# Tables formed ahead of the weight stream, the order of the end, and an output pair ahead of the gated unit's products, in a two-block float32 kernel

## The chip, the cores and the metric

The program runs on one core of one Trainium2 chip. The metric is the device time of one execution in microseconds (us), the median of the runs shown. TensorE is called PE here, VectorE DVE, ScalarE ACT, GpSimd POOL and SyncE SP.

## The reference, cut to what matters

One sequence of 256 tokens with 1024 channels passes through a first block of two layers and a second block of one. All arithmetic is float32.

```
for layer in range(2):                       # first block
    xn = rms_norm(h, attn_norm_g); proj = xn @ w_in          # [256,1024] @ [1024,2304]
    u_ssm, u_g, v_g, q, k, v = split(proj, 256,256,256,512,512,512)
    y_ssm  = s5_mixer(u_ssm, ...)      # complex diagonal scan over tokens, GELU,
                                       # y * sigmoid(y @ w_glu + b_glu)  (the gated unit)
    y_sgu  = u_g * (W_s rms_norm(v_g) + b)                   # spatial gating
    y_diff = differential attention (q, k normed and rotated, 4 heads)
    h = h + concat(y_ssm, y_sgu, y_diff) @ w_out
    h = h + (gelu(conv3(gate)) * conv3(val)) @ w_down        # up 5632 wide, down 2816 deep
# second block
x = x + rms_norm((gates_a*ya + gates_b*yb + gates_m*ym) @ w_out, g_post)
# ya: attention over 3 dilated windows (24 heads, q and k rotated), yb: grouped attention,
# ym: attention over 256 memory rows; each times silu(gate) and a branch projection
```

## The kernel before, in words

**The stream.** The weights of both blocks are cut into chunks of 512 (or 256) columns and these into pairs, 294 in all, 512 KB each. A pair has a slot number p in `STREAM`: in layer 0 q has 0 to 3, k 4 to 7, ssm_u 8 and 9, gmlp 10 to 13, v 14 to 17, and the two output chunks 18 to 25 in turns. SP loads pair p into one of 7 `raw` buffers (L415) when pair p-7 has been used. ACT makes the high part of it (`whi`, L1068, `hi_upto(n)`: all up to pair n-1), DVE the low part (`wlo`, raw minus whi, L1662, `lo_upto(n)`), and PE then multiplies three products per piece: high by high, low by high, high by low (L534 to L536 where one token tile is done at a time, `tile_pairs`; L571 to L573 and L578 to L580 in `project`). PE waits for whi and wlo of each pair; `emptied(name)` waits until the PSUM bank of the chunk has been read out.

**The order.** Each engine runs one list in order, written out by hand; `hi_upto` and `lo_upto` are put between the other work. `link` on DVE and POOL makes the next instruction wait for the one before.

**The start.** POOL forms the scale of token tile t (`norm_rstd`, L1501 to L1503), DVE scales (`norm_scale`, L1671), PE transposes (L625), ACT and DVE write the high and low parts (`norm_hi` L1088, `norm_lo` L1680). PE does pairs 0 and 1 of q for tile 0, transposes the state matrices (L636, `b_transposes`), does pair 2, transposes tile 1, pair 3, and then q for tile 1, for which `norm_lo(0, 1)` must have run. Meanwhile DVE forms phases (L1716 to L1730, `phase_turns` L341 to L343), the rotation rows (`ropeq`, four instructions with `link`, L1773) and `coefficients` (L1740 to L1754). POOL forms powers of the decay (`amplitude_powers` L1526 to L1529), then `input_powers` (L395 to L398, for two halves c=0, 1), `head_powers` (L1537, L1538, L1490, L1491), `decay_table`, the identity sums and skip rows (L1558 to L1560, L1508; they overwrite the mask constants, so they wait for `maskb_ready`), `fold_coefficient` (L372 to L374) and `output_powers` (L383 to L385).

**The mixing of a layer.** PE: q, k, ssm_u, transposes of q heads (L730), `shuffle_in` (L668), `input_products` (L679, waits for ACT's `uc`), gmlp, transposes of k heads (L730, waits for DVE's scaled k, L1872), `scores(0)` (L744, L747), v, and so on. Then `output_products` (L689, L695; L689 waits for the transposed probabilities that ACT copies out, L1218), `shuffle_out`, `values`, `glu_products` (L717, the gated unit's), the output chunks.

**The second block.** In the rotations of six chunks (`rot_terms` on DVE L2120, two instructions per token tile; POOL adds them, L1628 and L1629; PE transposes the result, L965) and the branch attentions (ACT exponentials, DVE `branch_division` L2125 and L2127, PE transposes L936) the steps are placed by slot number n; `bm_slot(n, lag)` says whether attention step d has its stage with this lag at n. At the end PE does the branch chunks, transposes the first half of `merged` (L1035), does pairs 0 and 1 of wo0, transposes the second half, does pairs 2 and 3 of wo0, then wo1. DVE writes the low parts of the transposed `merged` (L2233, which PE's wo0 waits for), after the gating of the last branch (L2223, L2230). When the sums of squares are there, POOL forms the scale (L1502, L1503), DVE multiplies (L2245) and adds (L2250) and SP stores (L473).

Of the kernel before, what the change touches and what calls it, by code (L numbers as in the profile page):

```python
# [136 lines left out]
def build(nc, weights, x, mem, cols, rows, lams, bmerge, consts, amask, bexp, cexp, wst, wglu, out):  # L137
    with ExitStack() as ctx:
# [107 lines left out]
        st_ = sbt(mix, "st_", [P, 3, 8, 4])  # L246
        sv = qh[:, :, :, :].rearrange("p a b (s c) -> p (a b s) c", c=NC).rearrange("p (k s) c -> p k s c", k=4)
# [155 lines left out]
        def _(sp):  # L403
# [3 lines left out]
            n_par, n_id = COL["conv"][0], CST["ident"][1]  # L407
# [3 lines left out]
            for p, (nm, j) in enumerate(STREAM):  # L411
# [105 lines left out]
        def _(pe):  # L517
# [141 lines left out]
            for l in range(LAYERS):  # L659
# [186 lines left out]
                if l == 0:  # L846
# [106 lines left out]
            for c, nm in enumerate(A_CHUNKS):  # L953
                for j in range(4):
                    project(nm, pairs=[j], fm=nm == "ga")
                    if 1 <= c <= 6 and j >= 2:

                        rnd = 2 * (c - 1) + j - 2
# [3 lines left out]
                        for i in range(2):  # L962
                            f = 2 * (j - 2) + i
                            for t in range(TT):
                                m = pe.transpose(S1[:, i * TOK + t * P:i * TOK + (t + 1) * P], rt[:, t, f * P:(f + 1) * P], ident)  # L965
# [92 lines left out]
        def _(act):  # L1058
# [75 lines left out]
            act.wait_ge(sem("cst_landed"), 32)  # L1134
            act.copy(identb[:, :], ident).then_inc(sem("maskb_ready"), 1)
            for t, k in ((0, 4), (1, 2)):
                act.copy(maskb[:, t, :].rearrange("p (h n) -> p h n", h=k),
                         wide(cs("mdiff")[:, 0:128] if t == 0 else cs("mdiff")[:, 128:384], k)).then_inc(sem("maskb_ready"), 1)

            for l in range(LAYERS):  # L1140
# [32 lines left out]
                hi_upto(s0 + 17)  # L1173
                if l == 0:
                    phase_tables(act, 0)
# [1204 lines left out]
```

## Time and profile before

| what | us |
|---|---|
| median of 3 runs (1023.01, 1028.09, 1028.82) | 1028.09 |
| the profiled execution's own time | 1030.31 |
| span of its instructions | 1028.50 |
| mean granted clock of TensorE | 0.986 |

The span runs from the first to the last recorded instruction; the execution's own time is 1.81 us longer. Times in the rows are counted from the start of the span. A row of the timeline gives the start, the duration of the whole row (all its instructions), the engine, line, operation and tiles, the count (x3), and in brackets how long the engine sat idle before it and for what.

### The profile page before, as it was taken

What the parts mean: (1) busy time and instruction counts of PE and PEld (TensorE: products, weight loads), DVE (VectorE), ACT (ScalarE), POOL (GpSimd) and SP (SyncE); (2) the same over time, 40 slices, a digit from 0 to 9 for tenths busy, and PEclk for the clock granted to TensorE, in tenths of its full rate; (3) what the DMA queues carried; (4) which work ended last, traced back from release to release, by engine and by line L of the source; (5) the groups of instructions that cost most, each with busy time, mean ns of one, the idle gap of its engine ahead of it and who ended that gap; (6) DMA issues with size and microseconds to landing.
All of it is one profiled execution on the core that took longest, in us unless ns stands there. A gap on an engine that the chain in (4) does not pass through costs nothing.

```text
span 1028.5 us, 15910 instructions
## 1 busy us (share of the span) xinstructions
PE 988.0 (96%) x6210; PEld 862.9 (84%) x6214; DVE 703.5 (68%) x1072; ACT 547.7 (53%) x898; POOL 250.5 (24%) x196
## 2 busy tenths in 40 slices
PE   6979999999999999999999999999999999999986
PEld 4868889999977887889999888999767688888865
DVE  6998456699954688557787844648575755666955
ACT  7655545666654646546665634544445455555613
POOL 5880102588400021102435100012131300000210
PEclk9998899999999999999999999999999999999989
DMA  7632255556554543256655555565544445654541
GB/s 287 206 94 70 65 182 180 178 176 185 184 183 149 177 147 123 84 184 194 185 182 181 187 171 170 197 205 170 161 134 135 137 145 176 185 168 149 164 143 62
DMA packets 48474, 165.97 MB, mean 161 GB/s; under 512 B 6544, under 2 KB 7056, under 8 KB 48400
## 3 DMA queue, kind: packets, MB, share of 16 engines
q1 hardware_dynamic: 48400, 164.95, 50.6%
q8 instruction: 50, 0.82, 0.3%
q14 instruction: 24, 0.20, 0.1%
HBM read 162.83 MB, written 1.05 MB: 159 GB/s over the span
## 4 chain that ended last, share of the span: by engine, by line
PE 78%; DVE 13%; ACT 3%; issue 2%; POOL 2%; DMA 1%; SPq 0%; DVEq 0%; POOLq 0%; ACTq 0%
PE PJ L578 12%; PE PJ L580 11%; PE PJ L579 11%; PE PJ L571 10%; PE PJ L572 10%; PE PJ L573 10%; DVE wlo L1662 4%; PE PJ L534 2%; PE PJ L536 2%; PE PJ L535 2%; PE PJ L695 1%; ACT whi L1068 1%; DMA raw<-weights_in 1%; PE T L1009 1%; DVE xn L2120 1%
## 5 line engine op out<-in xcount | busy, mean ns | idle before, releaser
L1662 DVE TENSOR_TENSOR wlo<-raw,whi 128x1024 fp32r<-128x1024 f32 x294 | 377.6, 1313 | 125.1 <-ACT whi L1068 124.5
L1068 ACT ACTIVATE whi<-raw 128x1024 fp32r<-128x1024 f32 x294 | 303.4, 1061 | 71.5 <-DMA raw<-weights_in 65.3
L571 PE MATMUL PJ<-xth,whi 128*128 128x256 f32 x864 | 245.3, 284 | 1.7 <-DVE wlo L1662 0.9
L572 PE MATMUL PJ<-xtl,whi 128*128 128x256 f32 x864 | 244.5, 283 | 0.0
L573 PE MATMUL PJ<-xth,wlo 128*128 128x256 f32 x864 | 244.5, 283 | 0.0
L578 PE MATMUL PJ<-whi,xth 128*128 128x512 f32 (+1 forms) x432 | 176.2, 408 | 8.9 <-DVE wlo L1662 3.9
L580 PE MATMUL PJ<-whi,xtl 128*128 128x512 f32 (+1 forms) x432 | 168.8, 391 | 0.0
L579 PE MATMUL PJ<-wlo,xth 128*128 128x512 f32 (+1 forms) x432 | 168.6, 390 | 0.0
L571 PEld LDWEIGHTS PJ<-xth,whi 128*128 128x128 f32 x864 | 165.8, 192 | 2.6 <-issue 2.4
L572 PEld LDWEIGHTS PJ<-xtl,whi 128*128 128x128 f32 x864 | 165.8, 192 | 0.2
L573 PEld LDWEIGHTS PJ<-xth,wlo 128*128 128x128 f32 x864 | 165.8, 192 | 0.0
L1587 POOL TENSOR_TENSOR gtd<-acc 128x512 f32<-128x512 f32 x22 | 81.9, 3725 | 153.0 <-ACT acc L1294 149.7
L578 PEld LDWEIGHTS PJ<-whi,xth 128*128 128x128 f32 x432 | 82.0, 190 | 30.6 <-issue 11.7
L2001 DVE SCALAR_TENSOR_TENSOR acc<-PJ,colv,acc 128x255 f32<-128x255 f32 (+1 forms) x176 | 72.2, 474 | 48.8 <-ACT acc L1289 48.2
L580 PEld LDWEIGHTS PJ<-whi,xtl 128*128 128x128 f32 x432 | 82.1, 190 | 17.7
L1289 ACT ACTIVATE acc<-PJ,colv 128x256 f32<-128x256 f32 x88 | 42.6, 564 | 100.4 <-PE PJ L573 100.4
L579 PEld LDWEIGHTS PJ<-wlo,xth 128*128 128x128 f32 x432 | 82.4, 191 | 14.8
L578 PE MATMUL PJ<-whi,hth 128*128 128x512 f32 x144 | 57.2, 397 | 0.2 <-ACT whi L1068 0.2
L579 PE MATMUL PJ<-wlo,hth 128*128 128x512 f32 x144 | 57.1, 396 | 0.0
L580 PE MATMUL PJ<-whi,htl 128*128 128x512 f32 x144 | 57.1, 396 | 0.0
L1641 POOL TENSOR_TENSOR merged<-merged,gt 128x512 f32<-128x512 f32 x6 | 10.6, 1787 | 160.9 <-DVE gt L2223 160.9
L1078 ACT ACTIVATE sqs<-xres 128x512 bf16<-128x512 f32 x20 | 12.7, 633 | 38.8 <-DVE xres L1975 36.3
(398 smaller groups left out, 1399.6 us busy)
## 6 DMA issues: line engine op xcount, KB each, us to landing
raw<-weights_in SPq DMA_DIRECT2D x294, 512.0 KB, 3.5
rt<-bmerge_in SPq DMA_DIRECT2D x6, 256.0 KB, 4.0
xres<-x_in SPq DMA_DIRECT2D x2, 512.0 KB, 5.2
xn<-mem_in SPq DMA_DIRECT2D x2, 512.0 KB, 5.5
y_out<-xn SPq DMA_DIRECT2D x4, 256.0 KB, 2.4
rowv<-rows_in SPq DMA_DIRECT2D x1, 576.0 KB, 10.7
ptmp<-bexp_in SPq DMA_DIRECT2D x2, 256.0 KB, 6.1
cex<-cexp_in SPq DMA_DIRECT2D x2, 256.0 KB, 8.4
```

The lines of the kernel that those rows point to most:

```text
L534: pe.matmul(o, h, wh, start=(j == 0 and kk == 0), stop=False, skip_group_check=True)
L571: pe.matmul(o, a, xh[:, k, :], start=(first and f % 2 == 0), stop=False, skip_group_check=True)
L572: pe.matmul(o, a, xl[:, k, :], start=False, stop=False, skip_group_check=True)
L573: m = pe.matmul(o, b, xh[:, k, :], start=False, stop=last, skip_group_check=True)
L578: pe.matmul(o, h, wh, start=first, stop=False, skip_group_check=True)
L579: pe.matmul(o, h, wl, start=False, stop=False, skip_group_check=True)
L580: m = pe.matmul(o, lw, wh, start=False, stop=last, skip_group_check=True)
L1068: act.activation(whi[:, p % HIGHS, :], raw[:, p % LOADS, :], ACT.Copy).then_inc(hi_ready, 1)
L1289: act.activation(acc[:, j % 2, i, :], PJ[BUF[c]][:, i // 2, (i % 2) * TOK:(i % 2 + 1) * TOK], ACT.Identity, scale=colv[:, k + 2:k + 3], bi ...
L1587: pool.tensor_tensor(gtd[:, j % 2, :, :], acc[:, j % 2, 0:2, :], acc[:, j % 2, 2:4, :], ALU.mult).then_inc(sem("gated"), 1)
L1662: dve.tensor_tensor(wlo[:, p % LOADS, :], raw[:, p % LOADS, :], whi[:, p % HIGHS, :].bitcast(F32), ALU.subtract).then_inc(lo_ready, 1)
L2001: dve.scalar_tensor_tensor(out=acc[:, j % 2, i, sh:TOK], in0=PJ[BUF[c]][:, i // 2, (i % 2) * TOK:(i % 2 + 1) * TOK - sh], scalar=colv[:, k ...
```

## The change

It moves work, and changes the form of two steps. Nothing of the result is left out.
- The masks get a place of their own (in `kT`, loaded by one more DMA), so that POOL's identity sums and skip rows of layer 0 come first, before the powers.
- DVE of layer 0: phases and `phase_turns` come before the first scaling; rotation rows (`rotation_rows`) before `norm_lo(0, 1)`; `coefficients` before q's sums; the low parts of pairs are spread otherwise.
- POOL of layer 0: scale of tile 1 after `amplitude_powers`; fold and the first output powers before both `head_powers`.
- PE of layer 0: `b_transposes` after pair 0 instead of 1; gmlp pair 0 before `input_products`; `prob_transposes(0)` before pair 3 of v. ACT copies these probabilities out before the second exponentials.
- Both layers: pair 0 of the first output chunk before `glu_products`.
- Second block: `branch_division` before the low part and both tiles of `rot_terms` after it; PE transposes by token tile, so that the first tile needs half of the rotation.
- End: the low parts of the first half of `merged` before the last branch; wo0 as pair 0, transposes, pairs 1 to 3; DVE multiplies by `gpost` before the scale is there, and then scales and adds in one instruction.

```diff
@@ SP @@
-                    small(cst[:, n_id:NCST], consts[:, n_id:NCST], "cst_landed")
+                    small(cst[:, n_id:n_mask], consts[:, n_id:n_mask], "cst_landed")
+                    small(mdiff[:], consts[:, n_mask:NCST], "cst_landed")
@@ PE @@
-                    if l == 0 and j == 1:
+                    if l == 0 and j == 0:
                         b_transposes(0, B[:, 0, :])
...
                     shuffle_in()
+                    project("gmlp0", pairs=[0])
                     input_products()
-                    project("gmlp0", pairs=[0, 1])
+                    project("gmlp0", pairs=[1])
...
                     sgu_products()
+                    prob_transposes(0)
                     project("v0", pairs=[3])
-                    prob_transposes(0)
...
                 values(1)
-                glu_products()
                 out_terms = dict(ready=(sem("mix_lo"), 4 * l, 1), order=OUT_PAIRS)
                 project(f"out{l}_0", pairs=[0], **out_terms)
+                glu_products()
...
-                        pe.wait_ge(sem("a_rope"), 4 * c)
+                        pe.wait_ge(sem("a_rope"), 4 * c - 2 + 2 * t)
...
-            project("wo0", ready=(sem("m_lo"), 0, 1), pairs=[0, 1])
+            project("wo0", ready=(sem("m_lo"), 0, 1), pairs=[0])
             for f in range(4, KD):
                 merge_transposes(f)
-            project("wo0", ready=(sem("m_lo"), 0, 1), pairs=[2, 3])
+            project("wo0", ready=(sem("m_lo"), 0, 1), pairs=[1, 2, 3])
@@ ACT @@
+            b_evac(0, PJ[buf("k0")][:, 0, :])
             hi_upto(4)
-            b_evac(0, PJ[buf("k0")][:, 0, :])
...
                 hi_upto(s0 + 20)
+                if l == 0:
+                    prob_evac(0)
                 for c in range(2):
                     exps(1, c)
@@ POOL @@
             link(pool.memset(mT[:], 0.0))
-            norm_rstd(0)
+            norm_rstd(0, (0,))
+            pool.wait_ge(sem("ident_landed"), 16)
+            link(pool.tensor_tensor(skip[:, 0:64], ident[:, 0:64], ident[:, 64:128], ALU.add))
...
+            skip_rows(0)
             pool.wait_ge(sem("par_ready"), 3)
             amplitude_powers()
+            norm_rstd(0, (1,))
             pool.wait_ge(sem("bex_ready"), 1)
             input_powers(pool, link, 0, 0, x_tile(0), ptmp)
             input_powers(pool, link, 0, 1, x_tile(1), ptmp)
-            head_powers(0, 0)
...
-            folded(0)
+            pool.wait_ge(sem("par_ready"), 4)
+            fold_coefficient(pool, link, 0, ptmp)
+            output_powers(pool, link, 0, 0, ptmp)
+            head_powers(0, 0)
             head_powers(0, 1)
-            output_powers(pool, link, 0, 0, ptmp)
             output_powers(pool, link, 0, 1, ptmp)
@@ DVE @@
             dve.sem_inc(sem("par_ready"), 1)
+            link(dve.tensor_scalar(v[19], v[5], 2.0 / math.pi, None, ALU.mult))
...
+            phase_turns(dve, link, 0)
             norm_scale(0, xres, 0)
             lo_upto(1)
-            norm_lo(0, 0)
-            lo_upto(2)
             dve.wait_ge(sem("par_a"), 4)
...
+            norm_lo(0, 0)
             lo_upto(3)
             norm_scale(0, xres, 1)
             lo_upto(4)
-            link(dve.tensor_scalar(v[19], v[5], 2.0 / math.pi, None, ALU.mult))
...
-            norm_lo(0, 1)
-            lo_upto(7)
-            dve.wait_ge(sem("cst_landed"), 32)
+            dve.wait_ge(sem("cst_landed"), 48)
...
+            rotation_rows(0)
+            norm_lo(0, 1)
+            lo_upto(6)
...
+                    if bm_slot(n, 2) is not None:
+                        branch_division(bm_slot(n, 2))
                     lo_upto(F2 + n + 3)
                     if j == 0 and 1 <= c <= 6:
-                        rot_terms(c - 1, (0,))
-                    if bm_slot(n, 2) is not None:
-                        branch_division(bm_slot(n, 2))
-                    if j == 0 and 1 <= c <= 6:
-                        rot_terms(c - 1, (1,))
+                        rot_terms(c - 1, range(TT))
...
+                if i == 5:
+                    merged_lo(0)
+                    merged_lo(1)
                 lo_upto(min(end_pair(nm) + 3, FIRST[chunk("wo0")] + 3))
...
+                for t in range(TT):
+                    dve.wait_ge(sem("ssq_ready"), 24 + 2 * i + t + 1)
+                    dve.tensor_tensor(xn[:, t, half], PJ[buf(f"wo{i}")][:, t, :], gpost[:, half],
+                                      ALU.mult).then_inc(sem("wo_scaled"), 1)
...
+                        dve.scalar_tensor_tensor(out=xn[:, t, part], in0=xn[:, t, part], scalar=rstd[:, 6, t:t + 1],
+                                                 in1=xpar[t][:, part], op0=ALU.mult, op1=ALU.add).then_inc(sem("y_ready"), 1)
```

## Rows read from the trace of the kernel before

**Rows 1.** The page: busy time, share and count of each engine.
```profile
PE 988.0 (96%) x6210; PEld 862.9 (84%) x6214; DVE 703.5 (68%) x1072; ACT 547.7 (53%) x898; POOL 250.5 (24%) x196
```

**Rows 2.** Waits of PE: for whom; us in total, times, longest us.
```profile
PE PJ L578 <- DVE wlo L1662: 3.9, 3, 3.2
PE PJ L578 <- issue: 3.2, 1, 3.2
PE S L965 <- POOL rt L1629: 2.8, 2, 1.4
PE T L936 <- DVE sm L2127: 2.5, 5, 0.9
PE PJ L689 <- ACT pT L1218: 2.5, 2, 2.0
...
PE S L730 <- DVE xn L1872: 1.6, 1, 1.6
...
PE PJ L578 <- DVE xtl L2233: 1.0, 1, 1.0
...
PE T L679 <- ACT uc L1172: 0.7, 1, 0.7
```

**Rows 3.** Stretches: us; PE, PEld, DVE, ACT, POOL busy; PEclk; DMA share; GB/s.
```profile
70.00:76.00 6.00, 4.97 (x15) 3.52 (x16) 5.65 (x15) 3.32 (x15) 3.54 (x3) 0.72 0.08 9
...
96.00:112.00 16.00, 15.87 (x94) 14.75 (x94) 5.59 (x11) 8.29 (x17) 0.00 (x0) 0.58 0.00 0
404.00:419.00 15.00, 14.35 (x124) 12.77 (x124) 7.80 (x16) 13.61 (x27) 0.00 (x0) 1.00 0.12 36
...
995.00:1003.00 8.00, 8.00 (x27) 6.29 (x26) 0.00 (x0) 0.00 (x0) 0.00 (x0) 0.67 0.25 76
```

**Rows 4.** Timeline of DVE, 5 to 12 and 20 to 34 us.
```profile
7.62 0.88 DVE L1671 TENSOR_SCALAR xn<-xres,rstd 128x512 f32<-128x512 f32 x2 [2.61 <-POOL rstd L1503]
...
20.81 2.16 DVE L1680 SCALAR_TENSOR_TENSOR xtl<-T,colv,xth 128x128 fp32r<-128x128 f32 x8 [1.21 <-ACT xth L1088]
22.89 5.41 DVE L1662 TENSOR_TENSOR wlo<-raw,whi 128x1024 fp32r<-128x1024 f32 x3
28.21 5.42 DVE L1773 TENSOR_TENSOR ropeq<-cst,rowv 128x128 f32<-128x128 f32 x4
```

**Rows 5.** Timeline of ACT, 11 to 20 us, and of POOL, 20 to 34 us.
```profile
17.73 0.59 ACT L1099 COPY bex<-PJ 128x512 f32<-128x512 f32 x1 [1.70 <-PE PJ L636]
...
20.06 1.53 POOL L396 TENSOR_TENSOR vm<-bex,apw 128x768 f32<-128x768 f32 x1
...
27.17 2.52 POOL L396 TENSOR_TENSOR kmT<-bex,apw 128x768 f32<-128x768 f32 x1
...
31.30 1.85 POOL L398 TENSOR_TENSOR kmT<-kmT,ptmp 128x768 f32<-128x768 f32 x1
```

**Rows 6.** Timeline of DVE, 46 to 76 us.
```profile
53.25 0.69 DVE L341 TENSOR_TENSOR md<-sp_,chunks 128x512 f32<-128x512 f32 x1
...
54.44 0.69 DVE L343 SCALAR_TENSOR_TENSOR md<-md 128x512 f32<-128x512 f32 x1
...
67.40 2.98 DVE L1662 TENSOR_TENSOR wlo<-raw,whi 128x1024 fp32r<-128x1024 f32 x1
```

**Rows 7.** Timeline of PE, 66 to 71 us.
```profile
70.52 0.47 PE L578 MATMUL PJ<-whi,xth 128*128 128x512 f32 x1 [3.17 <-DVE wlo L1662]
```

**Rows 8.** Timeline of PE, 752 to 758 us, and of DVE there.
```profile
753.37 0.48 PE L578 MATMUL PJ<-whi,xth 128*128 128x512 f32 x1
...
757.75 0.44 PE L965 MATMUL S<-cst,rt 128*128 128x128 f32 x2 [1.39 <-POOL rt L1629]
...
751.48 1.64 DVE L2127 TENSOR_SCALAR sm<-sm,sx 128x256 f32<-128x256 f32 x2
```

**Rows 9.** Timeline of DVE, the end of the span.
```profile
1023.07 1.41 DVE L2245 SCALAR_TENSOR_TENSOR xn<-PJ,rstd,gpost 128x512 f32<-128x512 f32 x2 [2.64 <-POOL rstd L1503]
1024.40 1.28 DVE L2250 TENSOR_TENSOR xn<-xn,vm 128x512 f32<-128x512 f32 x2
```

More of the change, by code:

```diff
@@ L956, in _ @@
                     if 1 <= c <= 6 and j >= 2:
-                        rnd = 2 * (c - 1) + j - 2
-                        pe.wait_ge(sem("a_rope"), 4 * c)
+                        t = j - 2
+                        rnd = 2 * (c - 1) + t
+                        pe.wait_ge(sem("a_rope"), 4 * c - 2 + 2 * t)
                         if rnd:
                             pe.wait_ge(sem("a_ev"), rnd)
[L962 to L965, printed above, removed]
+                        for f in range(4):
+                            m = pe.transpose(S1[:, f * P:(f + 1) * P], rt[:, t, f * P:(f + 1) * P], ident)
                         m.then_inc(sem("a_tr"), 1)
@@ L1491, in power, with norm_rstd @@
                 pool.tensor_tensor(out_, out_, mhalf[:, 0:n], ALU.pow).then_inc(sem(signal), 1)
-            def norm_rstd(n):
+            def norm_rstd(n, tiles=range(TT)):
                 if n not in AT_ONCE:
@@ L1497, in norm_rstd @@
                     link(pool.tensor_scalar(ssm1[:, n, :], ssq[:, n, 0:4:2], D * EPS, None, ALU.add))
-                for t in range(TT):
+                for t in tiles:
                     pool.wait_ge(sem("ssq_ready"), 4 * n + (2 * t + 2 if n in AT_ONCE else 3 + t))
@@ L1710, in _ @@
             dve.sem_inc(sem("par_ready"), 1)
+            link(dve.tensor_scalar(v[19], v[5], 2.0 / math.pi, None, ALU.mult))
+            link(dve.tensor_scalar(v[18], v[19], MAGIC, None, ALU.add))
+            link(dve.tensor_scalar(v[18], v[18], -MAGIC, None, ALU.add))
+            link(dve.tensor_tensor(v[19], v[19], v[18], ALU.subtract))
+            link(dve.memset(chunks[:, :], 1.0))
+            link(dve.tensor_tensor_scan(chunks[:, :], chunks[:, :], chunks[:, :], -1.0, ALU.mult, ALU.add))
+            phase_turns(dve, link, 0)
             norm_scale(0, xres, 0)
             lo_upto(1)
-            norm_lo(0, 0)
-            lo_upto(2)
             dve.wait_ge(sem("par_a"), 4)
@@ L1771, in _ @@
                 s0 = slot(f"q{l}")
-                for i, (g, tb_) in enumerate((("qg", cosv), ("qg", sinv), ("kg", cosv), ("kg", sinv))):
-                    link(dve.tensor_tensor(ropeq[:, i, :, :], tb_, wide(row(g, 64 * l, 64), TT), ALU.mult))
+                if l:
+                    rotation_rows(l)
+                else:
+                    coefficients()
                 lo_upto(s0 + (9 if l else 7))
@@ L1867, in _ @@
                 if l == 0:
-                    phase_turns(dve, link, 0)
                     lo_upto(s0 + 13)
@@ L1937, in _ @@
                                                None, ALU.mult))
[L1938 removed]
+                if l:
+                    lo_upto(s0 + 21)
                 dve.wait_ge(sem("sgu_done"), l + 1)
@@ L2212, in _, with merged_lo @@
             output_lo(5)
+            def merged_lo(i):
+                dve.wait_ge(sem("m_hi"), i + 1)
+                dve.scalar_tensor_tensor(out=xtl[:, 2 * i:2 * i + 2, :], in0=AUX[i][:, :].rearrange("p (f n) -> p f n", f=2),
+                                         scalar=0.5, in1=xth[:, 2 * i:2 * i + 2, :].bitcast(F32),
+                                         op0=ALU.mult, op1=ALU.subtract).then_inc(sem("m_lo"), 1)
             for i, b in enumerate(BRANCH_ORDER):
@@ L2230, in _ @@
                         dve.tensor_tensor(m, m, gt[:, t, at_:at_ + 512], ALU.add).then_inc(sem("merged_ready_dve"), 1)
-            for i in range(4):
-                dve.wait_ge(sem("m_hi"), i + 1)
-                dve.scalar_tensor_tensor(out=xtl[:, 2 * i:2 * i + 2, :], in0=AUX[i][:, :].rearrange("p (f n) -> p f n", f=2),
-                                         scalar=0.5, in1=xth[:, 2 * i:2 * i + 2, :].bitcast(F32),
-                                         op0=ALU.mult, op1=ALU.subtract).then_inc(sem("m_lo"), 1)
+            merged_lo(2)
+            merged_lo(3)
             lo_upto(NPAIRS)
```

90 lines of the change are left out of this document (44 added, 46 removed).

## The prediction, made before the change was run

> **What bounds the kernel now.** I read the page's busy shares first: PE is busy for 988 of 1028.5 us, DVE for 68% [rows 1]. So only PE's idle time, and time in which PE runs at the lower clock, can be won. The waits of PE say where it idles [rows 2]: once 3.2 us for a low part of v's first pair, 2.0 for the transposed probabilities, 1.6 for the scaled k and 0.7 for `uc`, all in layer 0; 1.4 twice for a rotation and 0.95 twice for a division in the second block; 3.2 and 1.0 at the end. The stretches show the clock [rows 3]: 0.72 over 70 to 76 us, behind the wait of 3.17; 0.58 over 96 to 112, behind that of 2.0; 0.67 over 995 to 1003, behind that of 3.23 (1.2 GHz in part, 2.4 GHz in the rest). The same mixing stretch of layer 1, 404 to 419, had 1.00. Last come the timelines of DVE and POOL in the start, where the change moves most [rows 4, 5].
>
> **The change part by part.**
>
> *First scaling.* DVE sat idle for 2.61 us before 7.62 [rows 4]. It now gets six small instructions (some 1.4 us, by 0.2 each with their links) and `phase_turns`, 53.25 to 55.13 or 1.9 us [rows 6]. That is 3.3 in a hole of 2.6, and POOL's five small identity instructions come between, so that PE starts 0 to 1 late; I take 0.5. SP's added load costs its queue less than 1 us, ahead of pairs that are not due.
>
> *Rotation rows ahead of `norm_lo(0, 1)`.* This is the dear one. Before, the low parts of tile 1 began at 20.81 [rows 4] and PE's tile 1 just behind. The three low parts behind them took 5.41 where one takes 1.2, and the four rotation rows, 128x128 each, took 5.42, or 1.36 each. Beside them POOL ran `input_powers`, where an instruction took 1.53 alone and 2.52 beside a low part [rows 5]: the two engines take turns, one whole instruction each. A scaling by `tensor_scalar` is held up too: two of 128x256 took 1.64 [rows 8]. The change sends POOL into `input_powers` some 4 us earlier (amplitude powers need DVE's `par_ready`, now sent at 11 instead of 15; ACT's copy of the transposed state matrices, at 17.73 [rows 5], comes 2.4 earlier), at 16. That copy now stands ahead of the high part of pair 2, which I put at 16.8. Between this and `norm_lo(0, 1)` DVE has two low parts, two scalings and four rotation rows, 4.0 us of its own; POOL has six products of 1.53 to 1.85 and two copies of 0.4 less what is past, 9.6 us. By turns that ends at 16.8+4.0+9.6, or 30.4, against 20.81: 9.6 late, of which 0.2 may be hidden, so +9.4 for PE. The bounds: if DVE always came first, the rows would take 0.2 each and hide in the 1.21 us for which DVE waits for ACT there, so 0; if each of the eight DVE instructions met the longest whole turn, 8x1.85, or 14.8. I take 9.4, because rows 4 show turns wherever both were busy.
>
> The Trainium skill's page "SBUF — State Buffer", section "Who interferes with whom", says that a DVE instruction with two SBUF inputs and a GpSimd instruction that reads SBUF exclude each other for a whole instruction, and that the order of issue decides who waits. By it the sum could be 9.4 or near nothing, as the issues fall; the rows 4 and 5 show that it was DVE that paid on the long ones.
>
> *To the end of `scores(0)`.* It ended at 67.35, which is 70.52 less the wait [rows 7]. The wait for `uc` (0.7) is covered by gmlp pair 0, that for k (1.6) by DVE being rid of `phase_turns`: -2.3. DVE's chain from `norm_lo` on (two low parts, `coefficients`, sums, rotation, now beside POOL's output powers of some 2.5 us each) brings the low part of pair 9 about 1.5 late: +1.5. PE will also stand idle for 4 to 5 us before tile 1, longer than any pause that lowered the clock before, and PE has 24 wide products then; after 3.23 us the clock stayed low for some 6 us, after 3.17 for some 3 [rows 3], so I give +1 here, less than they cost there since DVE sets the pace behind it. With the 0.5 of the start and the 9.4, `scores(0)` ends 10.1 later, at 77.4.
>
> *From `scores(0)` to the output.* The wait of 3.17 for the low part of v's first pair goes: DVE's low part that took 2.98 beside POOL [rows 6] is done before `scores(0)` ends. What is late next is the low part of pair 15, behind `batch_max(0)` and the lambdas: +1.6. The 2.01 for the probabilities goes, since ACT copies them before the second exponentials, which wait for DVE anyway. With no pause ahead of the narrow products the clock should stay at 2.4 GHz, as in layer 1: 16x(1-0.58), or 6.7, and 6x(1-0.72), or 1.7, are won [rows 3]; 1.1 comes from small waits and issue gaps between. Sum -3.2-2.0-6.7-1.7-1.1+1.6, or -13.1. Bounds: -5 if the clock falls all the same, -16 without the new wait and with 0.7 of gaps more.
>
> *Output pair ahead of the gated unit.* Both need `g_ready`, the bank's release as much as the products, so PE waits for nothing new. The gated unit ends 2.8 us later; its result is due at the output pair with `mix_lo` 2, but DVE's `diff_norm(0)`, which stands between and waits for POOL, is not done earlier anyway. 0 in each layer, -0.4 to +1.5.
>
> *Second block.* At chunks 2 and 5 the division came behind a `rot_terms` and was held up by POOL; now ACT's exponentials are done before the low part's own wait ends. The transposes for tile 0 need only POOL's first half. PE's products that began at 753.37 could have begun at 751.8, and the transposes at 757.75 at 756.2 [rows 8]: 3.1, twice, -6.2. Bounds -5.1 (the recorded waits 0.95, 0.23 and 1.39 alone, twice) and -6.4. The division now waits for ACT ahead of the low part; DVE was idle for ACT there. Without that cover it would cost 1.0 in each of twelve places, of which PE sees none while low parts run two pairs ahead.
>
> *End.* PE began wo0 3.23 late; now its first low part is written before DVE's last two of the stream, and pair 0 covers the gating of the last branch (2.6 us for 2.8 of products). The wait goes, the 0.98 for the second half too, and the clock: 8x(1-0.67), or 2.6, and 0.3 before 995. Sum -7.1 [rows 2, 3]. Bounds -4 (a gap of some 1.5 stays and costs some clock) and -7.3.
>
> *Tail.* Behind the last scale DVE had four instructions, 1023.07 to 1025.68 [rows 9]; now two of 0.64 to 0.68: -1.3 (-0.6 to -1.4).
>
> Sum: +10.1-13.1+0-6.2-7.1-1.3 is -17.6. From the profiled execution's 1030.31 that is 1012.7; the median of the runs stands 2.2 lower, so I say 1010.5.
>
> **The rivals.** *The turns cost nothing* (chance 0.27). DVE's instructions slip in between POOL's and the rotation rows hide. For it: the fifteen small `coefficients` ran unhindered beside POOL's small ones; against it: rows 4. Then +9.4 and the clock's +1 and the +1.5 go: 1010.5-11.9, or 998.6.
>
> *The mixing's clock falls anyway* (chance 0.12). PE's narrow products behind `output_products` keep the clock down whatever is before them. Against: layer 1's 1.00 [rows 3]. Then 8.4 stay: 1018.9.
>
> *Slower: the pause at the start brings the clock down for the whole of k and ssm_u* (chance 0.04). PE then does some 25 us of products at 1.2 GHz, +25 less 6 that the DVE chain hides there: 1029.5; it decides the sign from about 18 us at the lower clock on. For it: no pause in the trace is as long as this one; against: after every pause of rows 3 it came back within 3 to 15 us.
>
> **How the numbers follow.** My forecast has 0.57. The time is the likeliest's, 1010.5. The range reaches from the first rival's 999 to the second's 1019, and leaves out some 0.15. A measurement here tells about 1% from no change: faster by over 1% (below 1017.8) takes the forecast, the first rival and a part of the second, 0.91; within 1% 0.06; slower 0.03.
>
> **What would show each step.** Right: PE's wait at tile 1's first product of q for DVE's xtl, 5 us or more, with rotation rows of 1 us and more beside `input_powers`; no wait for the low part of v's first pair; clock 1.00 over the narrow products; no wait of 3 us at wo0; no waits for division and rotation at chunks 2 and 5. Wrong: rotation rows of 0.2 each (first rival), or a clock of 0.6 in the mixing (second).

## The result, and the profile after

The changed kernel took 1013.58 us in the median of 4 runs (1013.32 to 1013.89), the kernel before, beside it, 1028.45 (1023.01 to 1029.48): a ratio of 0.987, 95% interval 0.983 to 0.990. The profiled execution took 1013.32, with a span of 1011.5 and a mean clock of 0.995. It is faster by over 1%, as forecast, 3.1 us slower than the number forecast, and inside the range.

The page's busy times first, to be read beside [rows 1].

```profile
PE 977.9 (97%) x6214; PEld 855.5 (85%) x6214; DVE 706.6 (70%) x1072; ACT 547.6 (54%) x898; POOL 244.2 (24%) x196
```

PE is busy for 10.1 us less with the same products: that is time at the lower clock. The other 7 of the 17 us of the profiled executions are idle time. Which, the waits of PE show (us in total, times, longest), beside [rows 2]:

```profile
PE S L627 <- DVE xn L1680: 11.7, 6, 9.6
PE PJ L536 <- DVE xtl L1689: 5.4, 2, 4.2
PE PJ L536 <- issue: 3.1, 2, 2.4
PE PJ L580 <- issue: 2.0, 4, 0.6
PE PJ L580 <- DVE wlo L1671: 1.6, 2, 1.4
...
PE PJ L691 <- ACT pT L1221: 0.5, 1, 0.5
```

The groups of [rows 2] for the rotation, the division, the scaled k, `uc` and `merged` are gone. New are 4.2, 2.4 and (in a group of its own) 1.3 in the start, 1.4 for a low part at v's second pair, and two gaps a layer, 2.0 in all, of the group "L580 <- issue". The stretches answer to [rows 3]: us; PE, PEld, DVE, ACT and POOL busy; granted clock; DMA share; GB/s.

```profile
78.00:94.00 16.00, 14.62 (x91) 12.01 (x90) 15.37 (x34) 9.41 (x30) 2.13 (x2) 1.00 0.33 106
94.00:110.00 16.00, 15.66 (x129) 13.57 (x128) 8.29 (x19) 12.49 (x29) 0.00 (x0) 1.00 0.11 34
402.00:417.00 15.00, 14.20 (x123) 12.68 (x122) 8.15 (x16) 13.60 (x26) 0.00 (x0) 1.00 0.11 36
...
985.00:993.00 8.00, 8.00 (x40) 6.58 (x40) 6.47 (x8) 5.82 (x7) 0.00 (x0) 1.00 0.47 172
...
36.00:40.00 4.00, 4.00 (x19) 3.32 (x18) 3.01 (x9) 1.25 (x2) 2.22 (x3) 0.98 0.78 262
32.00:36.00 4.00, 4.00 (x11) 3.03 (x11) 3.76 (x11) 1.06 (x1) 0.00 (x0) 0.50 0.26 82
28.00:32.00 4.00, 1.30 (x3) 1.10 (x4) 3.93 (x10) 0.38 (x1) 2.77 (x5) 0.67 0.01 2
```

The narrow products of layer 0 (94 to 110) now run at 2.4 GHz, and so does the end; at the lower clock are now the first products of tile 1, from 30.7 to some 36 us. Their cause stands in the timelines of PE, DVE and POOL there (start, duration, and in brackets the idle time before), beside [rows 4, 5]:

```profile
19.86 0.47 PE L536 MATMUL PJ<-whi,xth 128*128 128x512 f32 x1 [2.37 <-issue]
30.70 0.79 PE L536 MATMUL PJ<-whi,xth 128*128 128x512 f32 x1 [4.24 <-DVE xtl L1689]
...
8.90 0.93 DVE L1680 TENSOR_SCALAR xn<-xres,rstd 128x512 f32<-128x512 f32 x2 [0.46 <-POOL rstd L1510]
19.68 3.70 DVE L1680 TENSOR_SCALAR xn<-xres,rstd 128x512 f32<-128x512 f32 x2
24.66 5.35 DVE L1747 TENSOR_TENSOR ropeq<-cst,rowv 128x128 f32<-128x128 f32 x4
30.04 2.16 DVE L1689 SCALAR_TENSOR_TENSOR xtl<-T,colv,xth 128x128 fp32r<-128x128 f32 x8
45.83 1.21 DVE L1800 TENSOR_TENSOR qh<-PJ,ropeq 128x1024 f32<-128x1024 f32 x1
48.09 3.21 DVE L1671 TENSOR_TENSOR wlo<-raw,whi 128x1024 fp32r<-128x1024 f32 x1
...
23.61 2.51 POOL L397 TENSOR_TENSOR kmT<-bex,apw 128x768 f32<-128x768 f32 x1
26.09 1.56 POOL L398 TENSOR_TENSOR ptmp<-bex,apw 128x768 f32<-128x768 f32 x1
27.73 1.80 POOL L399 TENSOR_TENSOR kmT<-kmT,ptmp 128x768 f32<-128x768 f32 x1
...
44.78 2.97 POOL L385 TENSOR_TENSOR ptmp<-gpw,apw 128x1024 f32<-128x1024 f32 x1
```

The rotation rows took 1.34 each beside POOL's big products, and tile 1's low parts began at 30.04 instead of 20.81.

How the same points of PE's work moved between the two traces gives the account. A sum of the differences is the whole change of the profiled execution, 1030.31 to 1013.32.

| stretch | point at its end on PE, before and after | change in the stretch | forecast |
|---|---|---|---|
| first scaling | first product, 11.58 and 12.63 | +1.05 | +0.5 |
| to tile 1 | its first product, 21.47 and 30.70 | +8.18 | +9.4 |
| to `scores(0)` | its last product, 67.35 and 76.83 | +0.25 | +0.2 |
| mixing of layer 0 | first transposes of the next stage, 139.02 and 137.09 | -11.41 | -13.1 |
| layer 0's rest, layer 1's mixing | 432.86 and 431.55 | +0.62 | 0 |
| second block | `merged`'s transposes, 984.57 and 976.25 | -7.01 | -6.2 |
| end | last product, 1021.02 and 1005.26 | -7.44 | -7.1 |
| tail | own time, 1030.31 and 1013.32 | -1.23 | -1.3 |

### The profile page after: what moved, and what is told of

Read it like the earlier page. It is cut to its first block, busy times and chain, and to the rows that moved or that the text cites. A ratio compares the mean times of both kernels' runs of the same rounds, so it can differ in the third digit from the quotient of the medians.

```text
span 1011.5 us, 15918 instructions
## 1 busy us (share of the span) xinstructions
PE 977.9 (97%) x6214; PEld 855.5 (85%) x6214; DVE 706.6 (70%) x1072; ACT 547.6 (54%) x898; POOL 244.2 (24%) x196
## 3 DMA queue, kind: packets, MB, share of 16 engines
HBM read 162.83 MB, written 1.05 MB: 162 GB/s over the span
## 4 chain that ended last, share of the span: by engine, by line
PE 86%; DVE 7%; issue 2%; ACT 2%; POOL 1%; DMA 1%; DVEq 0%; POOLq 0%; SPq 0%; ACTq 0%
PE PJ L580 14%; PE PJ L582 13%; PE PJ L581 13%; PE PJ L573 10%; PE PJ L574 10%; PE PJ L575 10%; PE PJ L536 2%; PE PJ L538 2%; PE PJ L537 2%; DVE wlo L1671 2%; PE T L1011 1%; DVE xn L1680 1%; PE PJ L697 1%; PE T L1002 1%; PE T L775 1%
## 5 line engine op out<-in xcount | busy, mean ns | idle before, releaser
L580 PE MATMUL PJ<-whi,xth 128*128 128x512 f32 (+1 forms) x432 | 174.3, 403 | 3.9 <-issue 2.0
L580 PEld LDWEIGHTS PJ<-whi,xth 128*128 128x128 f32 x432 | 81.2, 188 | 24.9 <-issue 8.2
L580 PE MATMUL PJ<-whi,hth 128*128 128x512 f32 x144 | 57.2, 397 | 0.2 <-ACT whi L1070 0.2
L536 PE MATMUL PJ<-whi,xth 128*128 128x512 f32 x64 | 27.3, 426 | 8.5 <-DVE xtl L1689 5.4
```

The costliest lines, as they stand in the source:

```text
L536: pe.matmul(o, h, wh, start=(j == 0 and kk == 0), stop=False, skip_group_check=True)
L580: pe.matmul(o, h, wh, start=first, stop=False, skip_group_check=True)
```

## Experiments

The first eight kernels and `tail_back` start from the changed kernel or from `rot_late`; the last three build on what these showed. Where nothing else is said, each computes the whole reference.

### What the start costs: start_before

```diff
-            phase_turns(dve, link, 0)
             norm_scale(0, xres, 0)
...
+            norm_lo(0, 1)
+            lo_upto(7)
             dve.wait_ge(sem("cst_landed"), 48)
...
-            rotation_rows(0)
-            norm_lo(0, 1)
-            lo_upto(6)
```

and all else that the change moved ahead of `scores(0)` put back on PE, ACT, POOL and DVE. The masks keep their own place.

> The changed kernel with the start of the kernel before (order of DVE, POOL and ACT up to scores(0), transposed state matrices after pair 1, both gmlp pairs behind the input products); the mixing from scores(0) on, the output pair, the second block, the end and the tail stay changed. In the profile of the changed kernel PE does its first product of tile 1 at 30.70 us instead of 21.47, and ends scores(0) near 76.8 instead of 67.35. Theory (the new start costs and nothing behind needs it): scores(0) ends near 67.4 again, the time falls by about 9, less what comes back (3.2 for the low part of v's first pair if phase_turns in k's way makes it late again, with some 2 of clock behind it): 1004 to 1010. Rival (what the start costs it gives back later: rid of the start's tables DVE and ACT are ahead in the mixing): 1013 or more, with the waits for the low part of v's first pair and for the probabilities back and the clock down over the narrow products.

Measured: 1007.93 us (1007.84 to 1008.61), ratio 0.980 (0.977 to 0.984); 5.6 less than the changed kernel. The timeline of PE in it:

```profile
59.44 0.77 PE L732 MATMUL S<-cst,xn 128*128 128x128 f32 x5 [1.74 <-DVE xn L1881]
70.71 0.77 PE L580 MATMUL PJ<-whi,xth 128*128 128x512 f32 x1 [3.17 <-DVE wlo L1667]
```

`scores(0)` begins at 66.07 instead of 75.14, 9.1 earlier; the waits of 1.74 and 3.17 are back, and its stretch 70 to 76 had a clock of 0.50. By the first transposes after the output the lead is 4.9 (132.22 against 137.09). So the theory holds and the rival holds in part: the new start costs 9.1, and gives back 4.2 behind it. Many steps were put back at once here; the next kernels take single ones.

### Which instruction pays for POOL: rot_late and powers_wait

rot_late:

```diff
-            rotation_rows(0)
             norm_lo(0, 1)
             lo_upto(6)
+            rotation_rows(0)
```

> The changed kernel with the four rotation rows moved behind the low parts of tile 1 and of pairs 4 and 5, where POOL has finished input_powers. In the changed kernel they take 5.35 us at 24.66, beside POOL's input_powers, and PE waits for the low parts behind them. Theory (turns: each of the four waits for one whole POOL product): norm_lo of tile 1 starts 4 to 5 earlier, PE's wait there shrinks by as much, the rows take 0.2 to 0.4 each where POOL is done, and the time falls by 3 to 5, to 1008.5 to 1010.5. Rival (the price is POOL's, whatever DVE does there: the eight low parts of tile 1 are then held up by the same POOL products, by some 5 us): tile 1 is no earlier by more than 1 us and the time stays at 1013.

Measured: 1013.14 (1012.64 to 1013.56), 0.4 less than the changed kernel. The timelines of PE and DVE in it:

```profile
52.29 0.45 PE L573 MATMUL PJ<-xth,whi 128*128 128x256 f32 x1 [2.92 <-DVE wlo L1671]
...
24.89 2.15 DVE L1689 SCALAR_TENSOR_TENSOR xtl<-T,colv,xth 128x128 fp32r<-128x128 f32 x8
45.62 2.47 DVE L1805 TENSOR_TENSOR xn<-qh,sm 128x512 f32<-128x512 f32 x1
48.01 2.87 DVE L1806 TENSOR_TENSOR xn<-qh,sm 128x512 f32<-128x512 f32 x1
```

Neither theory gave this. The low parts of tile 1 were 5.2 earlier and PE's 4.24 were gone, as the theory of turns said, and the eight of them were not held up (2.15 beside a product of POOL from 23.85 to 26.35), against the rival; the time hardly moved, because DVE, now earlier in q's work, did two rotations beside POOL's output powers (2.47 and 2.87, where the same took 0.68 and 0.71 in the changed kernel), and PE waited 2.92 at ssm_u instead.

powers_wait:

```diff
             pool.wait_ge(sem("bex_ready"), 1)
+            pool.wait_ge(sem("xt_lo"), 16)
             input_powers(pool, link, 0, 0, x_tile(0), ptmp)
```

> The changed kernel with one wait added: POOL starts input_powers when the low parts of tile 1 are written (xt_lo 16). Nothing is left out. DVE then has no POOL product beside its scaling of tile 1, low parts of pairs 2 and 3 and rotation rows. Theory (turns): the four rotation rows take some 0.2 to 0.3 us each instead of 1.34, DVE's wlo pairs 1.2 instead of 2.0, tile 1's low parts start 5 to 7 us earlier, PE's wait of 4.24 goes; input_powers ends some 5 us later, which k's transposes and DVE's coefficients may feel. Time 1006 to 1010. Rival (rotation rows are slow by themselves, 128x128 with a broadcast operand): they still take 1.3 each with POOL idle, and the time stays within 1 us of 1013.5 or rises, since the powers are later.

Measured: 1015.23 (1013.07 to 1016.47), 1.7 more than the changed kernel; three of the four runs lie above all of its runs, one below. Its timelines of DVE and PE:

```profile
20.97 1.26 DVE L1748 TENSOR_TENSOR ropeq<-cst,rowv 128x128 f32<-128x128 f32 x4
27.34 1.46 DVE L1758 TENSOR_TENSOR sp_<-colv 128x16 f32<-128x16 f32 x1
...
40.27 0.77 PE L580 MATMUL PJ<-whi,xth 128*128 128x512 f32 x1 [4.13 <-DVE wlo L1672]
```

With POOL idle the four rotation rows took 1.26 together, 0.31 each: the 1.34 of the changed kernel is POOL's price, and the mechanism is shown. But the time did not fall, and in the median it rose. The `coefficients` behind them, 128x16 and 0.17 each in the changed kernel, now stood beside `input_powers`, and six of them took 1.41 to 1.67; PE then waited 4.13 and 3.11 for low parts of k and ssm_u. The turns were not saved but paid by the next in DVE's queue.

### The output powers: rot_late_heads_first

```diff
             input_powers(pool, link, 0, 1, x_tile(1), ptmp)
+            head_powers(0, 0)
...
             fold_coefficient(pool, link, 0, ptmp)
-            output_powers(pool, link, 0, 0, ptmp)
-            head_powers(0, 0)
             head_powers(0, 1)
+            output_powers(pool, link, 0, 0, ptmp)
```

on top of rot_late.

> As rot_late (rotation rows behind the low parts of tile 1), and POOL's head powers ahead of the decay table and of the output powers again, as in the kernel before. In rot_late the wait of 4.24 at tile 1 was gone, and 2.92 came at 52.29 us for a low part of ssm_u, behind a low part of 2.83 and two rotations of 2.47 and 2.87 which DVE did beside POOL's output powers. Theory (POOL's big products cost DVE their turns wherever they stand, and the output powers stand in q's way there): the rotations take 0.7 each, the wait at ssm_u goes or is under 1, and the time falls by 3 to 5 from 1013.1, to 1008 to 1010. Rival (DVE is late by its own work, with coefficients and phase_turns ahead of q's sums): the wait at ssm_u stays over 2 and the time is above 1012.

Measured: 1007.58 (1006.75 to 1008.50), ratio 0.981 (0.977 to 0.985), 5.6 less than rot_late. Its timeline of DVE:

```profile
42.86 0.70 DVE L1805 TENSOR_TENSOR xn<-qh,sm 128x512 f32<-128x512 f32 x1
43.48 0.69 DVE L1806 TENSOR_TENSOR xn<-qh,sm 128x512 f32<-128x512 f32 x1
```

The rotations are short, and no wait of 0.3 or more is left on PE between 25 and 72 us. The output powers, which began at 42.64 in rot_late, began at 55.16 here: ahead of the head powers they put POOL's longest products beside DVE's work on q. With the rotation rows already moved, taking them away won 5.6, and the whole price of the start is gone (start_before took 1007.93). The head powers' order without rot_late's edit was not run, so how the price divides between the two is not shown; rot_late alone won only 0.4.

### One pause and the narrow products: probs_late

```diff
-                    prob_transposes(0)
                     project("v0", pairs=[3])
+                    prob_transposes(0)
...
-                if l == 0:
-                    prob_evac(0)
                 for c in range(2):
                     exps(1, c)
-                if l:
-                    hi_upto(s0 + 21)
-                    prob_evac(0)
-                    hi_upto(s0 + 22)
+                hi_upto(s0 + 21)
+                prob_evac(0)
+                hi_upto(s0 + 22)
```

> The changed kernel with the transposed probabilities put back in layer 0: PE transposes them after pair 3 of v, ACT copies them out after the second exponentials. Theory (one pause of PE ahead of the narrow products brings the clock down for them): PE waits 1.5 to 2.5 us before output_products and the granted clock over the next 16 us falls to 0.55 to 0.8, so that the time rises by 2 plus 3 to 7: 1018 to 1022. Rival A (the clock needs the longer wait for v's first pair too, which stays away): the wait of about 2 comes back, the clock stays at 1.00, 1015.5. Rival B (ACT is early enough now that even the old order waits for nothing): 1013.5.

Measured: 1020.73 (7 runs, 1015.51 to 1022.41). PE's timeline and the stretch behind, of the profiled execution (1021.41):

```profile
99.65 0.52 PE L691 MATMUL PJ<-uc,mT 128*128 128x64 f32 x3 [2.01 <-ACT pT L1221]
```

```profile
99.00:115.00 16.00, 15.35 (x89) 14.84 (x91) 3.76 (x7) 8.27 (x16) 0.00 (x0) 0.57 0.01 1
```

The wait is the 2.01 of before, and the clock falls to 0.57 where the changed kernel has 1.00: the theory. What it did not foresee is that this is not so in each execution. Of the seven, five took 1020.5 to 1022.4 with a mean clock of 0.988 to 0.991, and two took 1015.5 and 1016.1 with 0.997: 2.2 us above the changed kernel, as the wait of 2.01 alone would give. None of the other six executions was traced; that the clock fell in four of them and stayed up in two is read from the mean clock.

### The output pair: glu_first

```diff
                 out_terms = dict(ready=(sem("mix_lo"), 4 * l, 1), order=OUT_PAIRS)
-                project(f"out{l}_0", pairs=[0], **out_terms)
                 glu_products()
+                project(f"out{l}_0", pairs=[0], **out_terms)
```

> The changed kernel with the gated unit's products ahead of the first output pair again, in both layers. In the changed kernel PE has two new gaps a layer, 0.34 and 0.64, at 109.32 and 115.12 and again at 414.97 and 420.77, and between 403.83 and 431.55 it loses 1.05 us against the kernel before. Theory (the swap costs about 1 us in each layer: the low part of the gated unit's result is later and the output pairs behind it wait): both gaps go in both layers and the time falls by 2 to 1011.6. Rival (the gaps belong to something else, the order of the low parts or the earlier probabilities in layer 0): they stay and the time is within 0.4 of 1013.6; then layer 1, where only the swap differs, should show them still.

Measured: 1011.50 (5 runs, 1011.21 to 1012.20), 2.1 less than the changed kernel, whose four runs lie in 1013.32 to 1013.89. First the changed kernel, layer 1, PE and ACT; then glu_first:

```profile
414.97 0.47 PE L580 MATMUL PJ<-whi,xth 128*128 128x512 f32 x1 [0.34 <-issue]
417.80 1.89 PE L719 MATMUL PJ<-md,wglus 128*128 128x256 f32 x8
420.77 0.47 PE L580 MATMUL PJ<-whi,xth 128*128 128x512 f32 x1 [0.64 <-issue]
...
419.73 0.84 ACT L1267 ACTIVATE md<-PJ,hb 128x256 f32<-128x256 f32 x2 [2.65 <-PE PJ L719]
```

```profile
416.33 0.59 PE L580 MATMUL PJ<-whi,xth 128*128 128x512 f32 x1
419.64 0.47 PE L580 MATMUL PJ<-whi,xth 128*128 128x512 f32 x1
...
416.91 0.85 ACT L1267 ACTIVATE md<-PJ,hb 128x256 f32<-128x256 f32 x2
```

The gaps go in both layers, and 403.8 to 431.55 shrinks by 1.08. The pair at 420.77 is the first of the second output chunk. It uses v's bank, in which the gated unit's products stand too, and waits (`tanh_ready` in `EMPTIED`) until ACT has read them: that ends at 420.57 when the products come behind the first pair, and at 417.76, with that pair's products for cover, when they come ahead. For the 0.34 at 414.97 the trace names no releaser.

### The second block and the end, one half each: div_late, low_late, tail_back

div_late:

```diff
-                    if bm_slot(n, 2) is not None:
-                        branch_division(bm_slot(n, 2))
                     lo_upto(F2 + n + 3)
                     if j == 0 and 1 <= c <= 6:
-                        rot_terms(c - 1, range(TT))
+                        rot_terms(c - 1, (0,))
+                    if bm_slot(n, 2) is not None:
+                        branch_division(bm_slot(n, 2))
+                    if j == 0 and 1 <= c <= 6:
+                        rot_terms(c - 1, (1,))
```

> The changed kernel with DVE's division of a branch attention back between the two halves of the rotation, behind the low part; the transposes by token tile stay. Theory (two causes, one half each): the waits of 0.95 and 0.23 for the division come back at chunks 2 and 5, with the pause of 0.15 that the order brings, and those of 1.39 for the rotation stay away: time up by 2.5 to 3.2, to 1016.5. Rival (the transposes by tile are enough, the division was only late because the transposes' order held PE up): 1013.6. Second rival (the division alone did it all: with it late, the second half of the rotation is late again too): all waits back, up by 6, to 1019.8.

Measured: 1017.74 (1017.35 to 1018.74), 4.2 more. First the changed kernel (PE and DVE), then div_late:

```profile
749.80 0.60 PE L939 MATMUL T<-cst,sm 128*128 128x128 f32 x4
752.99 0.60 PE L967 MATMUL S<-cst,rt 128*128 128x128 f32 x4
...
746.57 0.62 DVE L2146 TENSOR_SCALAR sm<-sm,sx 128x256 f32<-128x256 f32 x2
```

```profile
751.51 0.41 PE L939 MATMUL T<-cst,sm 128*128 128x128 f32 x2 [0.96 <-DVE sm L2146]
...
750.46 1.63 DVE L2146 TENSOR_SCALAR sm<-sm,sx 128x256 f32<-128x256 f32 x2
```

The waits for the division are back at both chunks, those for the rotation are not. So there are two causes, with the division's the larger: PE loses 3.8 us over the block where I had expected 2.5 to 3.2. At each of the two chunks it loses 1.57 with the division's waits, and 0.33 just before. The rotation's share is what is left; the kernel with that half alone put back was not run.

low_late:

```diff
-                if i == 5:
-                    merged_lo(0)
-                    merged_lo(1)
...
-            merged_lo(2)
-            merged_lo(3)
+            for i in range(4):
+                merged_lo(i)
```

> The changed kernel with the low parts of the first half of merged back behind the last branch's gating on DVE; PE's order of the end (pair 0, transposes, pairs 1 to 3) and the tail stay. Theory (the order on DVE is what won the end, and with the pause the clock): PE waits some 3 us before wo0 again and the clock falls to about 0.67 over the 8 us behind it; time up by 3.2+2.6 to 1019.4, less what pair 0 no longer hides. Rival (PE's new order is enough, as pair 0 covers the gating): no wait and 1013.6.

Measured: 1018.70 (1017.04 to 1020.44), 5.1 more. Its timeline of PE and a stretch:

```profile
986.49 0.47 PE L580 MATMUL PJ<-whi,xth 128*128 128x512 f32 x1 [3.23 <-issue]
```

```profile
985.00:993.00 8.00, 6.51 (x26) 5.33 (x27) 2.82 (x6) 1.46 (x3) 0.00 (x0) 0.79 0.24 74
```

The wait of 3.23 is that of before to the hundredth, and the clock falls behind it. From `merged`'s first transposes to the last product PE takes 36.5 us before, 34.0 here and 29.0 in the changed kernel. So DVE's order wins 5.0. Of the 2.4 that are left, PE's new order wins the wait of 0.98 for the second half. The other 1.4 is mostly clock: behind the same wait PE worked at 1.2 GHz for 5.8 us before and for 3.4 here, and whether the order or chance did that is not shown.

tail_back (the last scale, product and sum of before, L2245 and L2250):

> The changed kernel with the last scale, product and sum of before: four instructions of DVE behind each token tile's scale instead of two. Theory (two instructions of 0.64 to 0.68 less on the path that ends the kernel): the end of PE to the end of DVE grows from 3.48 to 4.66 us as in the kernel before, and the time by 1.2 to 1014.8. Rival (the stores of the output overlap the rest and the last one ends the kernel only by its own start, which is set by the second half of the tile): under 0.5.

Measured: 1015.12 (1015.05 to 1015.42), 1.5 more. The end of DVE in tail_back, then in the changed kernel, where two instructions are left behind the scale:

```profile
1007.91 1.41 DVE L2269 SCALAR_TENSOR_TENSOR xn<-PJ,rstd,gpost 128x512 f32<-128x512 f32 x2 [2.63 <-POOL rstd L1510]
1009.23 1.28 DVE L2274 TENSOR_TENSOR xn<-xn,vm 128x512 f32<-128x512 f32 x2
```

```profile
1006.41 0.69 DVE L2268 TENSOR_TENSOR xn<-PJ,gpost 128x512 f32<-128x512 f32 x1 [2.97 <-ACT sqs L1477]
1007.32 1.42 DVE L2278 SCALAR_TENSOR_TENSOR xn<-xn,rstd,vm 128x512 f32<-128x512 f32 x2 [0.21 <-POOL rstd L1510]
```

From the start of PE's last product to the end of DVE it is 4.66 us in tail_back and 3.48 in the changed kernel, 1.2 of the 1.5, as the theory said.

### Towards a better order: best_a, best_b, best_c

best_a is rot_late_heads_first with glu_first's edit. best_b adds

```diff
-                    if l == 0 and j == 0:
+                    if l == 0 and j == 1:
                         b_transposes(0, B[:, 0, :])
...
-            b_evac(0, PJ[buf("k0")][:, 0, :])
             hi_upto(4)
+            b_evac(0, PJ[buf("k0")][:, 0, :])
```

and best_c, on top,

```diff
                     batch_max(0)
-                    lambdas()
                     lo_upto(s0 + 17)
+                    lambdas()
```

> rot_late_heads_first with the gated unit's products ahead of the first output pair again in both layers. Theory (the two are independent: one frees DVE's queue in q and k, the other spares PE the wait for the bank that the gated unit's result is read from): 1007.6 less the 2.1 that glu_first gave, 1005.5. Rival (the gaps of the swap hide a wait that then shows, since PE comes to the output earlier by 7): 1007 or more.

> best_a with the transposed state matrices after pair 1 again and ACT's copy of them behind the high parts of pairs 2 and 3. In rot_late_heads_first PE waits 2.36, 1.30 and 0.75 between 17 and 25 us, and in start_before, with this order, it waits for nothing there. Theory (those waits come from the high part of pair 2 behind the copy, and from POOL's input_powers which start early and hold DVE's low part and scaling up): they go, PE is 3 to 4 earlier at k, and the time falls by 1.5 to 4, to 1001.5 to 1004. Rival (POOL's powers are then later and hold up DVE's low parts of tile 1 and of q, as in start_before where three low parts took 6.38): the gain is under 1, 1005.

> best_b with DVE's lambdas behind the low parts of pairs 15 and 16 instead of ahead of them. In the changed kernel PE waits 1.38 before v's second pair, in rot_late_heads_first 1.83, for a low part which stands behind batch_max(0) and the lambdas. Theory (the lambdas, some 1 us, are what is in its way): the wait falls to under 0.8 and the time by 0.6 to 1.2 against best_b. Rival (ACT's gate inputs, which wait for the lambdas, are then late and hold up the gating rows and the probabilities): the same time or slower by up to 2.

Measured: best_a 1005.73 (1004.46 to 1006.12), best_b 1005.03 (1003.59 to 1006.72), best_c 1003.04 (1002.45 to 1003.63), ratio 0.974 (0.973 to 0.976), against a before of 1028.39. best_a is 1.9 below rot_late_heads_first: the two edits add up. best_b misses its theory and fits its rival (0.7 lower, with overlapping runs). PE's waits between 17 and 25 us are gone, but the rows of DVE and PE show the price moved on again:

```profile
26.35 5.41 DVE L1747 TENSOR_TENSOR ropeq<-cst,rowv 128x128 f32<-128x128 f32 x4
...
36.49 0.77 PE L580 MATMUL PJ<-whi,xth 128*128 128x512 f32 x1 [3.38 <-DVE wlo L1671]
```

In best_c the wait of 1.38 at v became 0.73 and 0.41, and PE's point behind the output came 0.65 earlier (127.72 against 128.37); but `scores(0)` had begun 0.43 earlier already (67.07 against 67.50), which leaves the lambdas some 0.2. Its median is 2.0 lower, while the two profiled executions have the same span, 1001.8; where the 2.0 comes from is not shown. best_c is the fastest kernel of the study, 10.5 us below the changed one.

## Why the prediction came out as it did

**The sign and most terms.** The account of the profiled execution comes to -17.0 where the sum said -17.6. Of what was to show the steps right all was seen but one size: rotation rows of 1.34 beside `input_powers`, no wait for v's first low part, the clock at 1.00 over the narrow products, none of the waits at wo0 and at chunks 2 and 5. PE's wait at tile 1 was 4.24 where I wanted 5 or more, since another 4.4 came ahead of it, in waits of 2.37, 1.29 and 0.74 at pair 2, at tile 1's transposes and at pair 3. These are not the rotation rows' doing: rot_late, without the rows in the way, kept 3.5 of them, and best_b, with the state matrices transposed later, had none.

**First scaling** was +1.05, not +0.5: `phase_turns` and POOL's scale ran beside each other, and the three instructions of the scale took 0.74, 0.33 and 1.03 instead of 0.23, 0.19 and 0.57. Some of it is noise: PE's first transposes came between 9.04 and 9.77 in the kernels with this start, and at 8.78 in start_before, where the kernel before had them at 8.25 with the same order.

**Rotation rows ahead of `norm_lo(0, 1)`** was right in mechanism and size: +8.2 for +9.4, low parts at 30.04 for 30.4. powers_wait showed the price to be POOL's. The first rival, that the turns cost nothing, is refuted. But the reading behind the step was too narrow. I put the price on these four instructions; rot_late and powers_wait took it off them and the time stayed or rose, since another of DVE's instructions with two inputs in SBUF (the on-chip memory of the tiles; PSUM is the one PE writes) met POOL's products instead. What the start costs is how many of POOL's big products fall into the time in which DVE's queue holds PE up, and the change put the output powers there too. The Trainium skill's page "SBUF — State Buffer", section "Who interferes with whom", says that a DVE instruction with two SBUF inputs contends with a GpSimd instruction that reads SBUF, and that one with at most one SBUF input doesn't, outside the two-port performance modes. The rows of the changed kernel agree on both kinds: the row at 45.83 reads PSUM and took 1.21 within POOL's 44.78 to 47.75, while the low part at 48.09, with two SBUF inputs, took 3.21. But one SBUF input alone doesn't make an instruction safe: the two scalings of tile 1 at 19.68 took 3.70 beside POOL's products, and the same two took 0.88 in powers_wait, where POOL was idle. Whether they ran in such a mode no trace shows.

**To the end of `scores(0)`**: right in sum (+0.25 for +0.2), by two errors that cancel. The clock cost 2.7, not 1: PE worked at 1.2 GHz from 30.70 to some 36.1, and half of 5.4 us is lost. The low part of pair 9 was not late (+1.5 forecast; in two other profiles of this start, glu_first and low_late, PE waits 0.9 and 0.8 for it).

**From `scores(0)` to the output**: -12.5, when the 1.1 of the gated unit in layer 0 is taken out, for -13.1. probs_late shows that the term of 6.7 for the clock hangs on the pause before the narrow products (in five of seven executions), and start_before that it doesn't hang on the one before v's first pair, which was back there while 90 to 106 ran at 1.00. The rival that the clock falls anyway is refuted.

**Output pair ahead of the gated unit**: this step is wrong. "PE waits for nothing new" overlooked the second output chunk, whose bank holds the gated unit's products until ACT has read them. It costs 1.1 a layer, 2.1 in all; the bound was +1.5 a layer.

**Second block, end, tail**: -7.0, -7.4 and -1.2 for -6.2, -7.1 and -1.3. div_late and low_late split the first two: the division ahead of the low part is worth some 3.8 of the 7.0, DVE's early low parts 5.0 of the 7.4.

**The base** is the step that failed most. From 1012.7 by the sum I took 2.2 off, since the median of before stood that far below its profiled execution. The changed kernel's median stands 0.3 above its own. These 2.5, and the 0.6 by which the sum missed, are the 3.1 between 1010.5 and 1013.58. The runs show what was wrong with it. Of the 31 executions of the kernel before beside the experiments, six took 1022.2 to 1023.7 with a mean clock of 0.993 to 0.996, all others 1027.2 to 1031.2 with 0.983 to 0.991. The profiled one, 1030.31 with 0.986, is of the second sort, and its narrow products' clock of 0.58 is what the change removes. The median of 1028.09 is of the second sort too. So the 2.2 is not the step between the two sorts, but part of the 4 us over which the second is spread, where the changed kernel's four runs lie within 0.6. Within it the longer executions have mostly the lower mean clock (the twelve with 0.988 or more have a median of 1028.8, the thirteen others 1030.2), but no trace shows where it is lost. The change wins 17 against the profiled execution, and about 9 against one of the six. That it is the narrow stretch whose clock stayed up in those is read from the mean clock and from probs_late, not from a trace of them. Either way a shift within the runs of before can't be carried over to a kernel whose runs don't have that spread.

**The slower rival** (the pause at the start keeps the clock low for all of k) didn't come: after the 4.24 the clock was 0.50 over 32 to 36 us and 0.98 over 36 to 40.

Not settled: how the price of the start divides between the rotation rows and the output powers, what the 0.34 gap before the first output pair waits for, what the moved `phase_turns` and lambdas are each worth, and why DVE's instruction wins or loses a given turn against POOL's.

## What to carry to other kernels

Where two engines take turns at SBUF, don't price the instruction that is seen to suffer: moving it hands the turn to the next one. As rot_late_heads_first did, count the other engine's large instructions in the stretch in which the first engine's queue holds up PE, and move those out of it. Before work is put ahead of a stage, list what releases the banks of everything behind, not of the moved step alone. And when a trace shows a stretch at the lower clock, look whether every execution has it before its median is used as a base.

## What the runs showed of the hardware that was not expected

The clock doesn't fall behind a pause in each execution of one and the same program. With a pause of 2.01 ahead of narrow products five of seven had a mean clock of 0.988 to 0.991 and the other two 0.997, and the five took some 5.6 us more in the median (probs_late); in the kernel before 25 of 31 had 0.983 to 0.991. One execution of each kernel was traced, and in both of these the stretch stood at 0.57 or 0.58. How long the lower clock lasted differed too. Over narrow products (128x64, 128x63) its mean was 0.57 for 16 us after 2.01. Wide ones (128x512) ran at 1.2 GHz for 5.4 us after 4.24, and after the same wait of 3.23 for 5.8 us in the kernel before and for 3.4 us in low_late. What sets this length is not shown.

Small DVE instructions are not safe from POOL's large ones. Of the fifteen `coefficients` of 128x16, 0.17 to 0.25 each in the changed kernel, six took 1.41 to 1.67 beside `input_powers` in powers_wait, all of them products or sums of two tensors, while the nine others took 0.17 to 0.39.
